# Encoder layer with expert-choice MoE: the prompt's routing beside the sample's output tiles, the sample's top-k on two halves of 256 columns

## What is computed

```python
h = rms_norm(x, attn_norm_g)
q, k, v, cv, cg = split(h @ w_in)
attn = blocked_attention(rope(rms_norm(q)), rope(rms_norm(k)), v)
conv = conformer_conv(cv, cg, ...)                 # gate, depthwise conv, layer norm, silu
mixed = concat([rms_norm(attn, attn_out_g), rms_norm(conv, conv_out_g)])
x = x + mixed @ w_out
h = rms_norm(x, ffn_norm_g)
aff = softmax(w_router^T h, axis=experts)          # 16 experts
gate, idx = top_k(aff, cap)                        # per expert, cap = n / 8: 128 prompt, 64 sample tokens
x = x.at[idx].add(gate * (silu(h[idx] @ w_gate) * (h[idx] @ w_up)) @ w_down)
```

## Time and profile before

| | us |
|---|---|
| median of 3 runs | 2719.85 |
| lowest, highest run | 2719.53, 2720.38 |
| the profiled execution | 2717.68 |
| span of its trace | 2715.8 |
| TensorE busy in the span | 2555.2 (94%) |
| VectorE busy in the span | 1843.6 (68%) |
| ScalarE busy in the span | 1390.9 (51%) |

### The profile page before, as it was taken

How to read it: one execution, slowest core, us unless ns; L and a number is a source line. 1 busy time by engine, 2 the same in 40 slices (tenths; PEclk the granted TensorE clock), 3 DMA queues, 4 the chain that set the end, 5 groups by cost and what they waited for, 6 DMA issues and landing times.

```text
span 2715.8 us, 39949 instructions
## 1 busy us (share of the span) xinstructions
PE 2555.2 (94%) x15892; PEld 2337.9 (86%) x15892; DVE 1843.6 (68%) x2136; ACT 1390.9 (51%) x1683; POOL 392.9 (14%) x328
## 2 busy tenths in 40 slices
PE   6999799997994599999999999999999999999997
PEld 5888689986783599899998998989989899899996
DVE  5787899986435566676676766766667676676673
ACT  4223555667221356565565554655546555565553
POOL 3645791000000101010010100101101001010010
PEclk9999999998997799999999999999999999999999
DMA  4123000002223477687786777767768677677773
GB/s 151 34 63 87 8 1 1 1 1 102 109 108 101 157 231 247 222 260 230 239 254 224 251 232 244 252 218 258 244 225 260 221 248 247 231 251 225 244 244 105
DMA packets 348093, 477.37 MB, mean 176 GB/s; under 512 B 10000, under 2 KB 301200, under 8 KB 347792
## 3 DMA queue, kind: packets, MB, share of 16 engines
q1 hardware_dynamic: 340880, 449.74, 50.6%
q0 software_dynamic: 7040, 25.17, 3.8%
HBM read 449.71 MB, written 25.17 MB: 175 GB/s over the span
## 4 chain that ended last, share of the span: by engine, by line
PE 89%; DVE 5%; ACT 2%; issue 1%; DMA 1%; POOL 1%; SPq 0%; ACTq 0%; POOLq 0%; DVEq 0%
PE psum L1437 30%; PE psum L1439 13%; PE psum L1198 8%; PE psum L1199 8%; PE psum L1200 8%; PE psum L1314 5%; PE psum L1459 4%; PE psum L1460 4%; PE psum L1301 2%; PE psum L1289 2%; DVE conv L818 1%; PE psum L1390 1%; ACT probs L624 1%; PE psum L1422 1%; DVE wi_lo L845 0%
## 5 line engine op out<-in xcount | busy, mean ns | idle before, releaser
L1110 DVE TENSOR_TENSOR w_lo<-raw,w_hi 128x2048 fp32r<-128x2048 f32 x384 | 880.2, 2292 | 494.5 <-ACT w_hi L716 492.7
L1437 PE MATMUL psum<-xgT,w_hi 128*128 128x384 f32 x4096 | 1167.6, 359 | 4.5 <-issue 4.5
L1439 PE MATMUL psum<-xgT,w_lo 128*128 128x192 f32 x4096 | 1026.0, 250 | 0.0
L716 ACT CAST w_hi<-raw 128x2048 fp32r<-128x2048 f32 x384 | 733.4, 1910 | 332.6 <-PE psum L1460 332.6
L1439 PEld LDWEIGHTS psum<-xgT,w_lo 128*128 128x128 f32 x4096 | 783.2, 191 | 0.6
L1437 PEld LDWEIGHTS psum<-xgT,w_hi 128*128 128x128 f32 x4096 | 769.9, 188 | 5.5 <-issue 4.8
L507 POOL DMA_INDIRECT out_dram<-o_p,put_p x16 | 25.8, 1610 | 1545.2 <-ACT o_s L757 1545.2
L818 DVE SCALAR_TENSOR_TENSOR conv<-conv,colp 128x1024 f32<-128x1024 f32 (+1 forms) x210 | 236.7, 1127 | 4.0
L1198 PE MATMUL psum<-w_hi,hid_st 128*128 128x512 f32 x512 | 212.9, 416 | 0.0
L1459 PE MATMUL psum<-w_hi,hid_st 128*128 128x512 f32 x512 | 202.6, 396 | 0.0
L1460 PE MATMUL psum<-w_lo,hid_st 128*128 128x512 f32 x512 | 202.6, 396 | 0.0
(11 more groups left out here) (188 smaller groups left out, 3480.7 us busy)
## 6 DMA issues: line engine op xcount, KB each, us to landing
raw<-in_w_gate_dram SPq DMA_DIRECT2D x128, 1024.0 KB, 5.3
raw<-in_w_up_dram SPq DMA_DIRECT2D x128, 1024.0 KB
raw<-in_w_down_dram SPq DMA_DIRECT2D x128, 1024.0 KB, 4.9
wi_raw<-in_w_in_dram SPq DMA_DIRECT2D x56, 256.0 KB, 3.9
out_dram<-x SPq DMA_DIRECT2D x12, 512.0 KB, 2.6
h_rows<-h SPq DMA_DIRECT2D x12, 512.0 KB, 2.9
xin<-in_x_prompt_dram SPq DMA_DIRECT2D x8, 512.0 KB, 3.4
wo_raw<-in_w_out_dram SPq DMA_DIRECT2D x8, 512.0 KB, 6.4
```

Of the source, the lines that this page charges most:

```text
L716: act.copy(w_hi[:, j % SPLIT_SLOTS, :], raw[:, j % RAW_SLOTS, :]).then_inc(e_hi, 1)
L1110: dve.tensor_tensor(w_lo[:, j % SPLIT_SLOTS, :], raw[:, j % RAW_SLOTS, :], w_hi[:, j % SPLIT_SLOTS, :].bitcast(F32), ALU.subtract).then_in ...
L1437: pe.matmul(bank[:, 0:2 * CAP], w_hi[:, slot, w0:w0 + P], xgT[:, half, k, :], start=(k == 0), stop=False, skip_group_check=True)
L1439: last = pe.matmul(bank[:, 0:CAP], w_lo[:, slot, w0:w0 + P], xgT[:, half, k, 0:CAP], start=False, stop=(k == KD - 1), skip_group_check=True)
```

## The change

Softmax, top-k and merge are made apart for the prompt (`n = 0`) and the sample (`n = 1`). The prompt's part begins once tile 7's logits exist: softmax and affinity transposes stand in the round of tile 9, three of the sixteen top-k rounds beside tile 9, four beside tile 10, four beside tile 11, the last five behind the last tile's norm. The sample's table is no longer 16 rows of 512 columns but 32 rows of 256, so it takes eight rounds and a merge of its own. The router's matmul is turned round: `h2T` is the stationary operand, the router's 16 columns stream, and the logits come out with tokens in the partitions, so that the copy and the transposes back are gone. On TensorE the h2 transposes of tile t-1 now stand between the two halves of tile t's product, and the logits of t-1 behind its second half. ScalarE's Square of a tile stands ahead of its other steps. The gathers for expert 0 take the row numbers from `rows_p` and `rows_sg` without a copy; the prompt's rows are gathered and transposed while the sample's rounds run.

```diff
+SELECT = [(0, ROT_TILES, HALF, CAP_P), (ROT_TILES, TILES, N_SAMPLE // 2, CAP_S)]
+SEL_ROWS = 2 * NE
+ROUNDS_BESIDE = {ROT_TILES + 1: 3, ROT_TILES + 2: 4, ROT_TILES + 3: 4}
...
 # GpSimd
-            pool.wait_ge(sel_ok, 6)
+            pool.wait_ge(prompt_rows, 1)
+            prompt_h_stored(pool)
+            pool.indirect_dma_start(xg_p[:, :], None, h_rows, bass.IndirectOffsetOnAxis(ap=rows_p[:, 0:1], axis=0)
+                                    ).then_inc(gathered, 16)
+            pool.wait_ge(sample_rows, 3)
             y_stored(pool)
+            pool.indirect_dma_start(xg_s[:, :], None, h_rows, bass.IndirectOffsetOnAxis(ap=rows_sg[:, 0:1], axis=0)
+                                    ).then_inc(gathered_s, 16)
...
-            gather(0)
-            gather_pair(0)
 # ScalarE
+            for t in range(TILES):
+                if t >= 1:
+                    square_x1(t - 1)
+                if t == ROT_TILES + 1:
+                    exp_logits(0)
+                if t + 1 < TILES and t + 1 != EARLY:
+                    mix_high(t + 1)
...
+                if t >= 1:
+                    h2_turned(t - 1)
+                if t + 1 == EARLY:
+                    mix_high(EARLY)
+            square_x1(TILES - 1)
+            h2_turned(TILES - 1)
+            exp_logits(1)
 # VectorE
+            for t in range(TILES):
+                if t >= 1:
+                    residual(t - 1)
+                if t == ROT_TILES + 1:
+                    softmax_max(0)
+                if t == 1:
+                    out_norms(1, EARLY, TILES)
+                    mix_rows(EARLY)
+                if t >= 1:
+                    ffn_norm(t - 1)
+                if t == ROT_TILES + 1:
+                    softmax_sum(0)
+                if t + 1 < TILES:
+                    mix_low(t + 1)
+                if 1 <= t and t + 2 < TILES:
+                    mix_rows(t + 2)
+                if t == ROT_TILES + 1:
+                    by_expert(0)
+                if t in ROUNDS_BESIDE:
+                    rounds(0, done, done + ROUNDS_BESIDE[t])
+                    done += ROUNDS_BESIDE[t]
+            residual(TILES - 1)
+            ffn_norm(TILES - 1)
+            rounds(0, done, CAP_P // 8)
+            places(0)
+            softmax_max(1)
+            by_rank(0)
+            softmax_sum(1)
+            better(0)
+            by_expert(1)
+            rounds(1, 0, CAP_S // 8)
+            places(1)
+            by_rank(1)
+            better(1)
 # TensorE
-                        last = pe.matmul(psum[0:NE, 7, 0:P], wr_sb[:, k, :], h2T[:, k * P:(k + 1) * P],
+                    last = pe.matmul(logits_of(t, t + 1), h2T[:, k * P:(k + 1) * P], wr_sb[:, k, :],
...
+            mixed_transposes(0)
             for t in range(TILES):
+                if t + 1 < TILES and t + 1 != EARLY:
+                    mixed_transposes(t + 1)
+                out_half(t, 0)
+                if t >= 1:
+                    h2_transposes(t - 1)
+                if t == ROT_TILES + 1:
+                    affinity_transposes(0)
+                out_half(t, 1).then_inc(proj, 1)
+                if t + 1 == EARLY:
+                    mixed_transposes(EARLY)
+                if t >= 1:
+                    router(t - 1)
+            h2_transposes(TILES - 1)
+            router(TILES - 1)
+            pick_transposes(0)
+            affinity_transposes(1)
...
+            pe.wait_ge(gathered, 16)
             for k in range(KD):
+                last = pe.transpose(gathered_prompt()[:, k, :], xg_p[:, k * P:(k + 1) * P], ident[:, :])
+            last.then_inc(xg_pT, 1)
+            pick_transposes(1)
+            pe.wait_ge(gathered_s, 16)
+            for k in range(KD):
+                last = pe.transpose(psum[:, 2 + k // 4, k % 4 * P:(k % 4 + 1) * P], xg_s[:, k * P:(k + 1) * P], ident[:, :])
             last.then_inc(xg_T, 1)
```

More of the change, by code:

```diff
@@ new lines, in h2_turned, with exp_logits @@
+            def h2_turned(t):
+                act.wait_ge(h2_T, t + 1)
+                if t >= 1:
+                    act.wait_ge(logit, t)
+                act.copy(h2T[:, :], flat(psum[:, 5:7, :])).then_inc(h2T_ok, 1)
+            def exp_logits(n):
+                t0, t1 = SELECT[n][0:2]
+                act.wait_ge(l_sub, n + 1)
+                act.activation(e16[:, t0:t1, :], e16[:, t0:t1, :], ACT.Exp).then_inc(l_exp, 1)
+            mix_high(0)
+            for k in range(1, KD):
+                high_wo(k)
@@ new lines, in _ @@
+            for t in range(NU - 1 - NORM_UNIT, TILES):
+                conv_norm(t)
+            done = 0
+            for t in range(TILES):
[19 more added lines that the diff above has]
+                    done += ROUNDS_BESIDE[t]
@@ L1407, in _, with out_half @@
-            pe.transpose(psum[:, 0, SEL_ROWS:2 * SEL_ROWS], topf[:, :], ident[0:SEL_ROWS, 0:SEL_ROWS]).then_inc(selT, 1)
-            pe.wait_ge(merge, 1)
-            pe.matmul(psum[:, 1, 0:2 * NE], reversal, sel[:, :, NE:2 * NE], start=True, stop=True).then_inc(reversed_b, 1)
+            def out_half(t, half):
+                if half == 0:
+                    pe.wait_ge(mT_l, t + 1)
+                    if t:
+                        pe.wait_ge(x1_ok, t)
+                for k in range(KD):
+                    if t == 0 and half == 0:
+                        pe.wait_ge(wo_l, k + 1)
+                    last = product3(psum[:, 3 + half, :],
+                                    mT_hi[:, t % 2, k * P:(k + 1) * P], mT_lo[:, t % 2, k * P:(k + 1) * P],
+                                    wo_hi[:, k, half * 512:(half + 1) * 512], wo_lo[:, k, half * 512:(half + 1) * 512],
+                                    k == 0, k == KD - 1)
+                return last
@@ new lines, in h2_transposes, with router @@
+            def h2_transposes(t):
+                pe.wait_ge(h2_ok, t + 1)
+                if t:
+                    pe.wait_ge(h2T_ok, t)
+                for k in range(KD):
+                    last = pe.transpose(psum[:, 5 + k // 4, k % 4 * P:(k % 4 + 1) * P], h2[:, t % 2, k * P:(k + 1) * P], ident[:, :])
+                last.then_inc(h2_T, 1)
+            def router(t):
+                pe.wait_ge(h2T_ok, t + 1)
+                for k in range(KD):
+                    last = pe.matmul(logits_of(t, t + 1), h2T[:, k * P:(k + 1) * P], wr_sb[:, k, :],
+                                     start=(k == 0), stop=(k == KD - 1))
+                last.then_inc(logit, 1)
@@ new lines, in affinity_transposes, with pick_transposes @@
+            def affinity_transposes(n):
+                pe.wait_ge(a_ok, n + 1)
+                for i in range(SELECT[n][2] // P):
+                    last = pe.transpose(psum[0:SEL_ROWS, sel_bank(n), i * P:(i + 1) * P], aff_tok[n][:, i, :], ident[:, :])
+                last.then_inc(a_T, 1)
+            def pick_transposes(n):
+                cap = SELECT[n][3]
+                pe.wait_ge(picked[n], 1)
+                pe.transpose(psum[0:cap, sel_bank(n), 0:SEL_ROWS], top[n][:, :], ident[0:SEL_ROWS, 0:SEL_ROWS])
+                pe.transpose(psum[0:cap, sel_bank(n), SEL_ROWS:2 * SEL_ROWS], topf[n][:, :], ident[0:SEL_ROWS, 0:SEL_ROWS]
+                             ).then_inc(selT[n], 1)
+                pe.wait_ge(merge[n], 1)
+                pe.matmul(psum[0:cap, sel_bank(n), 0:2 * NE], reversal[0:cap, P - cap:P], sel[n][:, :, NE:2 * NE],
+                          start=True, stop=True).then_inc(reversed_b[n], 1)
```

332 lines of the change are left out of this document (152 added, 180 removed).

## The result

The changed kernel takes 2700.94 us (median of 4 runs, 2699.89 to 2702.27) where the kernel before takes 2719.69 (4 runs, 2718.92 to 2720.38): a ratio of 0.9931, 95% interval 0.9919 to 0.9943, or 18.75 us less. The forecast of 2690 had the side and the range right and the gain too large: 29.9 us forecast, 18.75 measured.

What follows compares the result with a forecast made beforehand. The chain from the last output tile to the first expert matmul, 80.8 us, sets the time; experts stay as long. Last residual 6.2 us later, the rest 34.3 shorter: 28.1 gained, 2690 us, range 2679 to 2704.

Steps and rivals of the forecast that it cites:

- tile 2's product later: TensorE waits inside tile 1's product for tile 0's h2; tile 2 starts at 700.8, 8.7 us late.
- nine routers (and transposes) shorter: Between tile 2's start and the last residual, nine routers at 1.02 instead of 1.85 us: 7.5 us less.
- other work in front of R: Tile 10's h2 transposes, 0.9 us, and four affinity transposes, about 0.4, moved ahead of the last residual.
- R: Start of the last tile's residual addition, 834.41 us in the kernel before; forecast 840.6.
- VectorE late at tiles 10 and 11: Rounds beside tiles make the residual about 2 us late at two tiles; 3.7 us charged, bounds 0 and 8.
- R moves: Start of the last tile's residual addition goes from 834.41 to 840.6 us, 6.2 later.
- landing: Sample's gather on GpSimd, ahead of the first expert matmul: 8.64 us, bounds 4.2 and 8.6.
- the router's loads are not hidden: Rival: loading 128 columns costs as much as streaming them, router stays 1.85 us a tile; 2698 us, chance 0.11.
- the dear one of the present gathers: Price taken for the sample's gather, 8.64 us, as splitting and loading of expert weights starts beside it too.
- the residual's lost cover: Rival: TensorE waits for VectorE's residual in some nine tiles, 51 us; 2741 us, chance 0.03.
- the rounds did shrink with their columns: Denied by a rival: sample rounds stay 2.16 us, costing 6.5; 2696 us, chance 0.08 together with late residuals.
- had they stood behind the last tile: Rival: the prompt's eleven rounds end up behind the last tile all the same, 24 us; 2714 us, chance 0.02.

Runs made afterwards that it cites:

- after: The changed kernel itself, as measured and profiled against the kernel before: 2700.94 us, ratio 0.9931.
- e3: Changed kernel with tile 0's h2 transposes behind tile 1's whole product and tile 2's mixing transposes: 2690.19 us.
- e8: Changed kernel with tile 0's h2 transposes behind tile 1's whole product and VectorE's weight subtractions held until the sample's gather instruction ends, two before its low part: 2683.63 us.
- e6: Changed kernel with no rounds beside tiles 9 to 11, all sixteen prompt rounds behind the last residual: 2721.24 us, single run.
- e2: Changed kernel with SyncE's expert weight loads from the fifth chunk on held until the sample's gather has landed: 2698.46 us, single run.
- e1: Changed kernel with VectorE's first weight subtractions held until the sample's gather has landed, prompt's low part made ahead of that wait: 2693.0 us.

## Why the prediction was right in its course and wrong in its sizes

The mechanism held: the time is set by when the first expert matmul comes, the rounds went behind the output tiles, and the experts did not move. The steps, by the profiled executions:

| step | forecast us | measured us |
|---|---|---|
| tile 2's product later | +8.7 | +9.2 |
| half clock in it | 0 | +1.6 |
| nine routers (and transposes) shorter | -7.5 | -2.2 |
| other work in front of R | +1.3 | +1.4 (what is left over) |
| VectorE late at tiles 10 and 11 | +3.7 | +3.6 (2.0 of it waits) |
| R moves | +6.2 | +13.6 |
| R to the start of the sample's gather | 33.6 | 32.5 |
| landing | 8.64 | 12.79 |
| landing to first matmul | 4.3 | 4.4 |
| R to the first expert matmul | 46.5 | 49.7 |

The -2.2 is nine times 14.67 - 14.43. That 3.6 stands beside 3.7 is partly luck: the forecast charged waits alone, and 1.6 of the 3.6 is the clock at tile 11.

**The step that failed most is the router:** "So 1.02 us, 0.83 less." It is 1.69, or 9 x 0.67 = 6.0 us of error in nine tiles, of which other pieces of the tiles gave 0.7 back. The row I took as nearest has the form 16*128: its weights fill 16 partitions, the router's fill 128. Its matmuls are also transposes, and the router's are products; no run varied one of the two alone. The rival *the router's loads are not hidden*, at 0.11, was what happened. By the rule of the Trainium skill that I set aside ("TensorE: Matmul & The Clock Gate", section "LDWEIGHTS (loading the stationary operand)"), 107 ns for 128 columns, the router came to an estimated 1.7 us and the sum 6 us longer: the trace of after, with 106 ns, agrees with it.

**The landing** of 8.64 us, "the dear one of the present gathers", was taken as the upper bound, and it was 4.15 too low. All of that is the instruction: 6.59 us against the 2.30 inside the 8.64. The way behind it was priced well, 6.34 before and 6.20 after. The row of 2.30 beside three subtractions was there to be read, but not that all three could hold one gather.

**The clock at tile 2** was priced at 0.65 us behind the wait of 6 us, and not again behind the router. With 16 columns a matmul it fell at tile 2 in eight of nine profiled executions (e3 was granted 0.50 from 692.3 to 696.0, e8 1.00 there with the same instructions); with up to 64 in none of three. What decides it stays open.

**Right:** the eight short rounds (866.07 to 876.87 us, 1.35 each, as forecast), the prompt's gather hidden behind them (ScalarE copies its transposes at 873.25), the Exp table (loaded at 855.48, nobody waits), prompt rows at R + 17.7 (forecast 17.9), waits at tiles 10 and 11 alone. **The rivals:** the residual's lost cover did not come, no tile from 3 to 8 waits; the rounds did shrink with their columns; and had they stood behind the last tile, e6 shows that it would have cost 20.3 us, not the whole 23.7, since the waits go with them.

**Luck:** the range held for other reasons than it was made for. Its upper end of 2704 added the router's bound and 6.5 us for rounds or residuals. The router's tiles used 5.3; rounds and residuals came as forecast; and the landing's 4.15 and the clock's 1.6, for which it had no room upward, took the place of the 6.5.

## What to carry to other kernels

Work moved beside a busy stage pays if only a few of its instructions end up late there: 23.7 us saved for 3.6. Take the price of a weight load from a row of the same form, in partitions as well as columns, and of the same operation. Where a GpSimd gather is on the critical path, look at what VectorE has queued in those microseconds: put instructions that read two SBUF operands behind the gather's instruction (5.6 us here), and try to hold big loads until the gathered rows have landed (2.9 us in the landing; e2, which held them alone, is one run, 2.5 us under the changed kernel).

## What was not expected of the hardware

- A gather's instruction of 0.96 us took 6.59 or 6.60 when three subtractions of two SBUF operands on VectorE had begun before it, in all seven kernels with that order, and it was not let in between the three. The gather of the kernel before was held by one of three and took 2.30, and so were gathers of 2.45 us in the changed kernel and 2.23 in e1; what makes the difference stays open. Beside the same subtractions its transfer was not slower (4.14 us in e8 from start to landing).
- The last part of the gather, behind its instruction, took 6.2 us in the changed kernel, where 361 GB/s were moved in all (887.20 to 893.30), and 3.3 in e2, where 159 were.
- The clock fell to 1.2 GHz at tile 2 behind sixteen router matmuls of 16 columns and an idle time of 1 to 2 us close to them, in eight of nine profiles, and in none of three where the same sixteen streamed up to 64 columns. The longer streams cost nothing: 1.69 us either way.
